# Gate, mixture and attention output kept feature-major in a two-layer trunk on one core

## Chip, core and metric

The kernel runs on one core of one Trainium2 chip. The metric is the device time of one execution in microseconds. Three runs of the kernel before took 431.66, 431.68 and 431.73 us; the median is 431.68 us.

## What is computed

The input is x with 256 tokens of 1024 features, float32. Layer 0 is a causal pooling layer, layer 1 an attention layer with 16 heads of 128 features. Both have a gate. Cut to what matters:

```python
# layer 0: windows 2, 4, 8, 16 over four groups of 512 features
h = rms_norm(x, norm0)
u, z = split(h @ w_in0, 2)                 # 2048 features each
mixed = einsum('bsgc,gcd->bsgd', pooled(u), w_pool0) * pool_scale0
x = x + (mixed * silu(z)) @ w_out0
# layer 1
h = rms_norm(x, norm1)
q, k, v, z = split(h @ w_in1, 4)           # 2048 features each
q, k = rope(rms_norm(q, q_norm1)), rope(rms_norm(k, k_norm1))   # by head
o = softmax(causal(q @ k.T / sqrt(128))) @ v
x = x + (o * silu(z)) @ w_out1
```

All 256 tokens lie in one attention block, so the learned choice of blocks selects nothing further.

## The kernel before

Every large product is made from three products of float32r: high part by high part, high by low, low by high. ScalarE makes the high part of each weight block by a copy (`weight_hi`, L367), VectorE the low part by a subtraction (`weight_lo`, L836). The weights pass through a ring of four slots. A block of 128 x 2048 weights is a granule, and TensorE takes the granules in a fixed order. Granule n = 4g+j belongs to layer 0 (group g of 512 features; j = 0, 1 for u and 2, 3 for z), 16 to 19 to the mixture by w_pool0, 20 to 27 to w_out0, 28+8g+j to layer 1 (pairs of j for q, k, v, z), and 60 to 67 to w_out1. A slot is free for the next high part when TensorE has used it (`w_used`).

`granule` (L599 to L601) is token-major: activations stand still, and 512 weight columns move. `u_granule` (L641 to L644) is feature-major: 128 x 128 weights stand still and 256 tokens move. The results of a group lie in two banks `acc[0]` or two banks `acc[1]`; four further banks `aux` take what is turned (transposed on TensorE, L654), the scores and the attention output.

Layer 0: z is token-major. ScalarE takes tanh with the token's rstd as its scale (L429), VectorE makes the gate from it and the product (L925). GpSimd builds the window sums (L306, L311) from u, VectorE the pooled values (L896) and their low part (L902). The mixture is token-major too; VectorE multiplies it with the gate (L949), and TensorE turns the result (`turn_y0`), since w_out0 needs it feature-major.

Layer 1: ScalarE copies q and k out, squares them by head (L496) and hands the mean (L500) to GpSimd, which makes the norm factors and the rope products (L330 to L348). VectorE adds the rope halves (L1009) and TensorE turns q and k. The attention of group g-1 is spread over the granules of group g (`attend`): scores, maximum on VectorE (`head_max`, L986 to L992), exp on ScalarE (L468, L470), turned probabilities, product with v (L755 to L757), scaling and gate on VectorE (`head_out`), and at the end of the group the turn of y1 (`turn_y1`).

The order of the work is written out by hand on each engine, with semaphores between engines. Every engine takes its list in order, so an instruction that waits holds up all that stands behind it. The queue of the weights issues 66 loads of 1 MB (and the first 2 MB in eight pieces) in this order.

## Time and profile before

| what | value |
|---|---|
| profiled execution, its own time | 431.68 us |
| its span, first to last instruction | 429.9 us |
| TensorE busy | 423.5 us |
| VectorE busy | 281.4 us |
| ScalarE busy | 231.0 us |
| GpSimd busy | 163.1 us |
| mean DMA rate | 175 GB/s |

Times in the profile count from the start of the span. Busy time of TensorE is modelled and overlapping; the start of one matmul to the start of the next is what a matmul costs in the stream. A group of the timeline gives the start, the length from first start to last end and the count. "Idle before" is the time in which the engine stood still just before, with what ended it.

### The profile page before, as it was taken

Reading aid. Unit: us, or ns where it says so; the run is one execution under the profiler, and the core shown is the slowest. Engines: PE = TensorE matmul, PEld = TensorE weight load, DVE = VectorE, ACT = ScalarE, POOL = GpSimd, SP = SyncE. Lnnn points to the kernel's source line nnn. Section 1 sums busy time; section 2 is a strip of 40 time slices with the busy share of each in tenths; the row PEclk is TensorE's granted clock in tenths of the full one; section 3 lists DMA queues with packets and bytes.
Section 4 is the critical chain, followed back from the end, with each engine's and each line's share of the span. In section 5 each row is a group of like instructions: output and inputs, shape, how many; then the busy total and the mean of one; then the engine's idle time right before and its main releaser. Section 6 shows DMA issues by size and latency. Waiting matters only on the chain.

```text
span 429.9 us, 5672 instructions
## 1 busy us (share of the span) xinstructions
PE 423.5 (99%) x2214; PEld 362.7 (84%) x2214; DVE 281.4 (65%) x340; ACT 231.0 (54%) x406; POOL 163.1 (38%) x111
## 2 busy tenths in 40 slices
PE   8999999999999999999999999999999999999997
PEld 8979898988888888888788888888888888888885
DVE  3866898688985544356664798447983579836532
ACT  5745545444554443578447765477654786546310
POOL 0077417267000000089804595055940559300000
PEclk9999999999999999999999999999999999999999
DMA  8987578645455747436833667236672355731002
GB/s 273 386 285 272 195 244 314 214 159 178 167 197 175 217 137 221 123 94 204 295 101 99 186 184 226 91 100 193 196 216 84 99 191 196 246 105 41 2 0 98
DMA packets 38026, 75.25 MB, mean 175 GB/s; under 512 B 1648, under 2 KB 1776, under 8 KB 38000
## 3 DMA queue, kind: packets, MB, share of 16 engines
q1 hardware_dynamic: 37280, 73.83, 52.8%
q10 hardware_dynamic: 720, 1.07, 0.8%
q8 instruction: 17, 0.28, 0.3%
q14 instruction: 9, 0.07, 0.0%
HBM read 73.84 MB, written 1.05 MB: 174 GB/s over the span
## 4 chain that ended last, share of the span: by engine, by line
PE 85%; POOL 7%; DMA 2%; DVE 2%; ACT 1%; SPq 1%; issue 1%; DVEq 0%
PE acc L599 23%; PE acc L601 22%; PE acc L600 22%; PE aux L654 4%; POOL wide L344 3%; PE acc L644 3%; PE acc L643 3%; PE acc L641 3%; DMA raw<-in_w_in_dram 2%; PE aux L738 2%; POOL k_s L337 1%; PE aux L745 1%; SPq L232 1%; PE aux L757 1%; PE aux L756 1%; PE aux L755 1%
## 5 line engine op out<-in xcount | busy, mean ns | idle before, releaser
L836 DVE TENSOR_TENSOR w_lo<-raw,w_hi 128x2048 fp32r<-128x2048 f32 x65 | 165.2, 2548 | 57.6 <-ACT w_hi L367 57.5
L367 ACT ACTIVATE w_hi<-raw 128x2048 fp32r<-128x2048 f32 x64 | 121.9, 1915 | 28.3 <-PE acc L601 21.7
L599 PE MATMUL acc<-w_hi,hT_hi 128*128 128x512 f32 x320 | 127.7, 399 | 1.0 <-DVE w_lo L836 1.0
L601 PE MATMUL acc<-w_hi,hT_lo 128*128 128x512 f32 x320 | 124.9, 390 | 0.0
L600 PE MATMUL acc<-w_lo,hT_hi 128*128 128x512 f32 x320 | 124.6, 389 | 0.0
L601 PEld LDWEIGHTS acc<-w_hi,hT_lo 128*128 128x128 f32 x320 | 60.1, 188 | 13.0
L599 PEld LDWEIGHTS acc<-w_hi,hT_hi 128*128 128x128 f32 x320 | 60.2, 188 | 12.9 <-DVE w_lo L836 1.4
L600 PEld LDWEIGHTS acc<-w_lo,hT_hi 128*128 128x128 f32 x320 | 60.2, 188 | 11.5
L599 PE MATMUL acc<-w_hi,aT_hi 128*128 128x512 f32 x160 | 63.7, 398 | 0.0
L601 PE MATMUL acc<-w_hi,aT_lo 128*128 128x512 f32 x160 | 62.4, 390 | 0.0
L600 PE MATMUL acc<-w_lo,aT_hi 128*128 128x512 f32 x160 | 62.3, 389 | 0.0
L601 PEld LDWEIGHTS acc<-w_hi,aT_lo 128*128 128x128 f32 x160 | 30.0, 188 | 6.4
L600 PEld LDWEIGHTS acc<-w_lo,aT_hi 128*128 128x128 f32 x160 | 30.1, 188 | 5.8
L599 PEld LDWEIGHTS acc<-w_hi,aT_hi 128*128 128x128 f32 x160 | 30.1, 188 | 5.8
L330 POOL TENSOR_TENSOR q_rstd<-qk_mean,minus_half 128x8 f32<-128x8 f32 x4 | 6.6, 1640 | 71.7 <-ACT qk_mean L500 71.7
L986 DVE TENSOR_SCALAR minus_scale<-q_rstd 128x2 f32<-128x2 f32 x16 | 4.3, 266 | 36.6 <-PE aux L738 36.6
L644 PE MATMUL acc<-hT_lo,w_hi 128*128 128x256 f32 x96 | 27.2, 283 | 0.0
L643 PE MATMUL acc<-hT_hi,w_hi 128*128 128x256 f32 x96 | 27.2, 283 | 0.0
L641 PE MATMUL acc<-hT_hi,w_lo 128*128 128x256 f32 x96 | 27.2, 283 | 0.0
L344 POOL TENSOR_TENSOR wide<-k_s,rope_tab 128x256 f32<-128x256 f32 x16 | 25.4, 1616 | 0.3
L318 POOL TENSOR_TENSOR mean<-sumsq 128x2 f32<-128x2 f32 x1 | 0.2, 195 | 65.7 <-ACT ysb L385 65.7
L468 ACT ACTIVATE probs<-aux,exp_bias,q_rstd 128x128 f32<-128x128 f32 x16 | 7.2, 450 | 32.3 <-DVE exp_bias L992 32.3
(125 smaller groups left out, 593.7 us busy)
## 6 DMA issues: line engine op xcount, KB each, us to landing
raw<-in_w_in_dram SPq DMA_DIRECT2D x46, 1024.0 KB, 5.5
raw<-in_w_out_dram SPq DMA_DIRECT2D x16, 1024.0 KB, 5.0
raw<-in_w_pool_dram SPq DMA_DIRECT2D x4, 1024.0 KB, 5.5
raw<-in_w_in_dram SPq DMA_DIRECT2D x8, 256.0 KB, 7.4
wide<-in_xT_dram ACTq DMA_DIRECT2D x4, 256.0 KB, 6.6
xs<-in_x_dram SPq DMA_DIRECT2D x1, 1024.0 KB, 7.7
out_dram<-ysb SPq DMA_DIRECT2D x4, 256.0 KB, 2.0
wide<-in_table_dram SPq DMA_DIRECT2D x1, 256.0 KB, 8.9
```

The source lines that it names most:

```text
L344: ins = pool.tensor_tensor(s4[:, t, :, a:a + half], v4[:, t, :, b:b + half], tab, ALU.mult)
L367: act.activation(w_hi[:, slot, :], raw[:, slot, :], ACT.Copy).then_inc(hi_made, 1)
L468: act.activation(probs[:, 0:P], aux[h % 2][:, 0:P], ACT.Exp, bias=exp_bias[:, h, 0:1], scale=q_rstd[:, g % 2, 0, h:h + 1], accum_out=row_s ...
L599: pe.matmul(a, shi, whi, start=first and k == 0, stop=False)
L600: pe.matmul(a, shi, wlo, start=False, stop=False)
L601: ins = pe.matmul(a, slo, whi, start=False, stop=last and k == GK - 1)
L641: pe.matmul(u_tile(f), wlo, shi, start=j == 0 and k == 0 and f % 2 == 0, stop=False, skip_group_check=True)
L643: pe.matmul(u_tile(f), whi, shi, start=False, stop=False, skip_group_check=True)
L644: ins = pe.matmul(u_tile(f), whi, slo, start=False, stop=end, skip_group_check=True)
L654: ins = pe.transpose(aux[dst_banks[f // 2]][:, c:c + P], src[:, t, f * P:(f + 1) * P], ident[:, :])
L738: pe.matmul(s[:, P:3 * P], qT[:, h, P:SEQ], kT[:, h, :], start=True, stop=True).then_inc(scores_ready, 1)
L836: dve.tensor_tensor(w_lo[:, slot, :], raw[:, slot, :], w_hi[:, slot, :].bitcast(F32), ALU.subtract).then_inc(w_split, 1)
```

## The change

z of layer 0, the mixture, z of layer 1 and the attention output become feature-major. A new helper `tile_of_two` makes a 128-feature tile of them: the low weights meet the high activations (256 columns), and the high weights meet both parts of the activations, which now lie side by side in memory (512 columns). The high parts' product goes into the lower 256 columns of a bank, that with the low activations into the upper 256. The two have to be added afterwards: ScalarE copies the upper part out, VectorE adds it to the lower. A feature-major z has the token's rstd along the columns, so it can't be the scale of an activation any more; VectorE multiplies with a spread copy, `rstd_half_b`, which TensorE spreads once per layer. Tanh comes after it, from SBUF. The scaling by the softmax's sum moves from the attention output to the probabilities before they are turned (`probs_norm`). The turns of y0 and y1 are gone. The z weights of layer 1 are stored in another layout by the host (`w_gate`), in pairs of tiles. The two halves of a bank pair in layer 1 alternate by `side`.

```diff
+        quad = [ctx.enter_context(nc.psum_tensor(f"quad{b}", [P, 4, COLS], F32)) for b in range(2)]
+        acc = [[quad[b][:, t, :] for t in range(TT)] for b in range(2)]
+        aux = [quad[1][:, 2, :], quad[1][:, 3, :], quad[0][:, 2, :], quad[0][:, 3, :]]
...
-                    act.wait_ge(tables_made, 1)
-                for t in range(TT):
-                    product_ready(act, t, 2 * g + 1, 4 * g + 3)
-                    act.activation(wide[:, t, g * COLS:(g + 1) * COLS], acc[1][t][:, :], ACT.Tanh,
-                                   scale=rstd_half[:, t:t + 1]).then_inc(tanh_made, 1)
+                for p in range(2):
+                    product_ready(act, p, 2 * g + 1, 4 * g + 3)
+                    if g > 0:
+                        act.wait_ge(gate_made, 2 * (g - 1) + p + 1)
+                    act.activation(lo_part[p], quad[1][:, 2 * p:2 * p + 2, SEQ:], ACT.Copy).then_inc(lo_copied, 1)
+                for p in range(2):
+                    act.wait_ge(z_made, 2 * g + p + 1)
+                    act.activation(lo_part[p], gateT[:, HPG * g + 2 * p:HPG * g + 2 * p + 2, :],
+                                   ACT.Tanh).then_inc(tanh_made, 1)
...
+            def y0_lo_part(g):
+                for p in range(2):
+                    product_ready(act, p, 8 + g, N_POOL + g)
+                    act.wait_ge(*((y0_summed, 2 * (g - 1) + p + 1) if g else (gate_made, 2 * (GROUPS - 1) + p + 1)))
+                    act.activation(lo_part[p], quad[g % 2][:, 2 * p:2 * p + 2, SEQ:], ACT.Copy).then_inc(lo_copied, 1)
...
+            def z_lo_part(g, p):
+                act.wait_ge(w_used, N_L1 + 8 * g + 6 + p + 1)
+                if g > 0 or p > 0:
+                    act.wait_ge(gate1_made, 2 * g + p)
+                act.activation(z_lo, quad[side(g, 3 + p)][:, 0:2, SEQ:], ACT.Copy).then_inc(z1_lo_copied, 1)
+            def tanh_z(g, p):
+                act.wait_ge(z1_made, 2 * g + p + 1)
+                act.activation(z_lo, gate1T[:, p], ACT.Tanh).then_inc(tanh1_made, 1)
...
+            def tile_of_two(out_, n, c, h, start, stop):
+                pe.matmul(out_[:, 0:SEQ], w_lo[:, n % RING, c:c + P], h[:, 0, :], start=start, stop=False,
+                          skip_group_check=True)
+                return pe.matmul(out_, w_hi[:, n % RING, c:c + P], h.rearrange("p a s -> p (a s)"), start=False,
+                                 stop=stop, skip_group_check=True)
...
+            def mix(g):
+                n = N_POOL + g
+                pe.wait_ge(w_split, n + 1)
+                pe.wait_ge(pooled_split, g + 1)
+                pe.wait_ge(*((u_made, 2 * GROUPS), (z_made, 2 * GROUPS), (y0_summed, 2), (y0_summed, 4))[g])
+                for f in range(HPG):
+                    for k in range(GK):
+                        ins = tile_of_two(quad[g % 2][:, f, :], n, k * COLS + f * P, aT[:, HPG * g + k], k == 0,
+                                          k == GK - 1)
+                    if f == 1:
+                        ins.then_inc(tile0_ready, 1)
+                ins.then_inc(w_used, 1)
...
-                pe.matmul(aux[3][:, 0:P], probsT[:, 0:P], v[0], start=True, stop=True)
-                pe.matmul(aux[3][:, P:2 * P], probsT[:, P:2 * P], v[0], start=True, stop=False)
-                pe.matmul(aux[3][:, P:2 * P], probsT[:, 2 * P:3 * P], v[1], start=False,
-                          stop=True).then_inc(o_ready, 1)
+                o = aux[3][:, 0:SEQ]
+                pe.matmul(o[:, P:SEQ], v[1], probsT[:, SEQ:3 * P], start=True, stop=False, skip_group_check=True)
+                pe.matmul(o, v[0], probsT[:, 0:SEQ], start=False, stop=True, skip_group_check=True).then_inc(o_ready, 1)
...
+            def gate_pair(g, p):
+                n = N_L1 + 8 * g + 6 + p
+                pe.wait_ge(w_split, n + 1)
+                pe.wait_ge(qkv_out[1 + p], TT * (g + 1))
+                for f in range(2):
+                    for k in range(KD):
+                        ins = tile_of_two(acc[side(g, 3 + p)][f], n, k * 2 * P + f * P, hT[:, k], k == 0, k == KD - 1)
+                ins.then_inc(w_used, 1)
...
-                    dve.wait_ge(tanh_made, TT * g + t + 1)
-                    gate = wide[:, t, g * COLS:(g + 1) * COLS]
-                    ins = dve.scalar_tensor_tensor(gate, gate, 1.0, acc[1][t][:, :], ALU.add, ALU.mult)
-                    ins.then_inc(gate_made, 1)
+                if g == 0:
+                    dve.wait_ge(tables_made, 1)
+                for p in range(2):
+                    dve.wait_ge(lo_copied, 2 * g + p + 1)
+                    z = gateT[:, HPG * g + 2 * p:HPG * g + 2 * p + 2, :]
+                    chain.done(dve.tensor_tensor(z, quad[1][:, 2 * p:2 * p + 2, 0:SEQ], lo_part[p], ALU.add))
+                    dve.tensor_tensor(z, z, rstd_half_b[:, :].unsqueeze(1).to_broadcast([P, 2, SEQ]),
+                                      ALU.mult).then_inc(z_made, 1)
+                for p in range(2):
+                    dve.wait_ge(tanh_made, 2 * g + p + 1)
+                    z = gateT[:, HPG * g + 2 * p:HPG * g + 2 * p + 2, :]
+                    dve.scalar_tensor_tensor(z, lo_part[p], 1.0, z, ALU.add, ALU.mult).then_inc(gate_made, 1)
...
+            def y0_out(g):
+                for p in range(2):
+                    dve.wait_ge(lo_copied, 2 * (GROUPS + g) + p + 1)
+                    if g >= 2:
+                        dve.wait_ge(y_split, 2 * (g - 2) + p + 1)
+                    y = y0[g % 2][:, 2 * p:2 * p + 2, :]
+                    dve.tensor_tensor(y, quad[g % 2][:, 2 * p:2 * p + 2, 0:SEQ], lo_part[p],
+                                      ALU.add).then_inc(y0_summed, 1)
+                for p in range(2):
+                    dve.wait_ge(y0_summed, 2 * g + p + 1)
+                    for f in (2 * p, 2 * p + 1):
+                        i = HPG * g + f
+                        ins = dve.scalar_tensor_tensor(y0[g % 2][:, f, :], y0[g % 2][:, f, :],
+                                                       gains[:, 2 * KD + i:2 * KD + i + 1], gateT[:, i, :], ALU.mult,
+                                                       ALU.mult)
+                    ins.then_inc(y0_made, 1)
...
+                y0_out(g)
+                weight_lo(N_POOL + 4 + g, (N_POOL + 4 + g) % RING)
+                y0_lo(g)
...
+            def probs_norm(g, h):
                 dve.wait_ge(exp_made, HPG * g + h + 1)
                 chain.done(dve.reciprocal(row_inv[:, h, :], row_sum[:, h, :]))
-                chain.done(dve.tensor_tensor(o_scale[:, h, :], row_inv[:, h, :], rstd_half[:, :], ALU.mult))
+                dve.tensor_scalar(probs[:, 0:P], probs[:, 0:P], row_inv[:, h, 0:1], 1.0, ALU.mult, ALU.mult)
+                dve.tensor_scalar(probs[:, P:3 * P], probs[:, P:3 * P], row_inv[:, h, 1:2], 1.0, ALU.mult,
+                                  ALU.mult).then_inc(probs_made, 1)
+            def y1_out(g, h):
                 dve.wait_ge(o_ready, HPG * g + h + 1)
-                dve.wait_ge(y_turned, 8 + 2 * g)
-                for t in range(TT):
-                    ins = dve.scalar_tensor_tensor(y1[:, t, h * P:(h + 1) * P], aux[3][:, t * P:(t + 1) * P],
-                                                   o_scale[:, h, t:t + 1], gate1[:, t, h * P:(h + 1) * P],
-                                                   ALU.mult, ALU.mult)
-                ins.then_inc(y1_made, 1)
+                if g > 0:
+                    dve.wait_ge(y_split, 8 + HPG * (g - 1) + h + 1)
+                dve.tensor_tensor(y1T[:, h, :], aux[3][:, 0:SEQ], gate1T[:, h // 2, h % 2, :],
...
+            def z_sum(g, p):
+                dve.wait_ge(z1_lo_copied, 2 * g + p + 1)
+                if g > 0:
+                    dve.wait_ge(y1_made, HPG * (g - 1) + 2 * p + 2)
+                if (g, p) == (0, 0):
+                    dve.wait_ge(rstd_b_made, 2)
+                z = gate1T[:, p]
+                chain.done(dve.tensor_tensor(z, quad[side(g, 3 + p)][:, 0:2, 0:SEQ], z_lo, ALU.add))
+                dve.tensor_tensor(z, z, rstd_half_b[:, :].unsqueeze(1).to_broadcast([P, 2, SEQ]),
+                                  ALU.mult).then_inc(z1_made, 1)
+            def gate_out(g, p):
+                dve.wait_ge(tanh1_made, 2 * g + p + 1)
+                dve.scalar_tensor_tensor(gate1T[:, p], z_lo, 1.0, gate1T[:, p], ALU.add, ALU.mult).then_inc(gate1_made, 1)
...
                 rope_sum(g, 1)
+                z_sum(g, 0)
                 w(7)
-                gate_z(g)
-                if attend:
-                    y1_lo(g - 1)
+                gate_out(g, 0)
```

The change also writes the lists in another order. VectorE in layer 0, between the weights of two groups (`w_lo`), before; L925 makes the gate, L896 and L902 the pooled values, L889 takes u out:

```order
L925 SCALAR_TENSOR_TENSOR wide<-wide,acc 128x512 [waits tanh_made] x2
L836 TENSOR_TENSOR w_lo<-raw,w_hi 128x2048 [waits hi_made] x2
L896 SCALAR_TENSOR_TENSOR k_s<-ysb,uT 128x1024 [waits window_summed]
L889 TENSOR_TENSOR uT<-acc,rstd_b 128x2x256 [waits pooled_made,tile0_ready]
L889 TENSOR_TENSOR uT<-acc,rstd_b 128x2x256 [waits w_used]
L836 TENSOR_TENSOR w_lo<-raw,w_hi 128x2048 [waits hi_made]
L902 TENSOR_TENSOR aT_lo<-k_s,aT_hi 128x1024 [waits pooled_hi]
L836 TENSOR_TENSOR w_lo<-raw,w_hi 128x2048 [waits hi_made]
```

The same place in the changed kernel, where L995 is the addition of the halves, L996 the multiplication and L1001 the gate:

```order
L910 TENSOR_TENSOR w_lo<-raw,w_hi 128x2048 [waits hi_made]
L971 TENSOR_TENSOR aT<-k_s,aT 128x4x256 [waits pooled_hi]
L910 TENSOR_TENSOR w_lo<-raw,w_hi 128x2048 [waits hi_made]
L995 TENSOR_TENSOR wide<-quad,probs_pair 128x512 [waits lo_copied]
L996 TENSOR_TENSOR wide<-wide,rstd_half_b 128x512 [waits dve_chain]
L995 TENSOR_TENSOR wide<-quad,second 128x512 [waits lo_copied]
L996 TENSOR_TENSOR wide<-wide,rstd_half_b 128x512 [waits dve_chain]
L1001 SCALAR_TENSOR_TENSOR wide<-probs_pair,wide 128x512 [waits tanh_made]
L1001 SCALAR_TENSOR_TENSOR wide<-second,wide 128x512 [waits tanh_made]
L910 TENSOR_TENSOR w_lo<-raw,w_hi 128x2048 [waits hi_made] x2
```

Two instructions have become six, at the same place among the weights.

ScalarE in a group of layer 1 with attention, before, from the copy of q to the mean of k. L489 copies a product out, L496 squares, L500 makes the mean, L468 and L470 are exp, L477 copies turned probabilities, L367 is `w_hi`:

```order
L489 ACTIVATE wide<-acc,rstd 128x512 [waits w_used]
L496 ACTIVATE wide,qk_sum<-wide 128x128 [waits q_out]
L496 ACTIVATE wide,qk_sum<-wide 128x128 x7
L500 ACTIVATE qk_mean<-qk_sum 128x8 [waits q_summed]
L367 ACTIVATE w_hi<-raw 128x2048 [waits w_used,raw_landed0]
L468 ACTIVATE probs,row_sum<-aux,exp_bias,q_rstd 128x128 [waits p_turned,bias_made]
L470 ACTIVATE probs,row_sum<-aux,exp_bias,q_rstd 128x256
L477 ACTIVATE probsT<-aux 128x384 [waits p_turned]
L367 ACTIVATE w_hi<-raw 128x2048 [waits w_used,raw_landed1]
```

In the changed kernel (L511 copies out, L518 squares, L523 is the mean, L490 and L492 exp, L499 the probabilities, L383 `w_hi`):

```order
L511 ACTIVATE wide<-quad,rstd 128x512 [waits w_used]
L518 ACTIVATE wide,qk_sum<-wide 128x128 [waits q_out]
L518 ACTIVATE wide,qk_sum<-wide 128x128 x3
L490 ACTIVATE probs_pair,row_sum<-quad,exp_bias,q_rstd 128x128 [waits p_turned,bias_made]
L492 ACTIVATE probs_pair,row_sum<-quad,exp_bias,q_rstd 128x256
L499 ACTIVATE probs_pair<-quad 128x384 [waits p_turned]
L518 ACTIVATE wide,qk_sum<-wide 128x128 [waits q_out]
L518 ACTIVATE wide,qk_sum<-wide 128x128 x3
L523 ACTIVATE qk_mean<-qk_sum 128x8 [waits q_summed]
L383 ACTIVATE w_hi<-raw 128x2048 [waits w_used,raw_landed0]
```

The exp of a head and the copy behind it now stand between the two halves of the squares. The same holds for k, with the exp of head 3.

## Rows read from the trace of the kernel before

**Rows 1.** The page, its first part: busy time of each engine
```profile
PE 423.5 (99%) x2214; PEld 362.7 (84%) x2214; DVE 281.4 (65%) x340; ACT 231.0 (54%) x406; POOL 163.1 (38%) x111
```

**Rows 2.** The cores: span and granted clock
```profile
core 0: 429.9 us, clock 1.000
```

**Rows 3.** Waits of TensorE: total, times, longest us
```profile
PE aux L654 <- DVE k_s L1009: 0.6, 1, 0.6
```

**Rows 4.** Timeline, TensorE: start us, length us, operation, count [idle before]
```profile
31.97 0.28 PE L641 MATMUL acc<-hT_hi,w_lo 128*128 128x256 f32 x1
...
43.49 0.40 PE L599 MATMUL acc<-w_hi,hT_hi 128*128 128x512 f32 x1
...
99.23 0.39 PE L599 MATMUL acc<-w_hi,aT_hi 128*128 128x512 f32 x1
...
110.12 1.04 PE L654 MATMUL aux<-ident,ysb 128*128 128x128 f32 x8
...
116.47 1.03 PE L654 MATMUL aux<-ident,ysb 128*128 128x128 f32 x8
...
267.43 1.04 PE L654 MATMUL aux<-ident,ysb 128*128 128x128 f32 x8
268.31 1.04 PE L654 MATMUL aux<-ident,k_s 128*128 128x128 f32 x8
...
321.35 1.04 PE L654 MATMUL aux<-ident,k_s 128*128 128x128 f32 x8
```

**Rows 5.** Groups of instructions: count, busy us, mean ns, idle before
```profile
L599 PEld LDWEIGHTS acc<-w_hi,hT_hi 128*128 128x128 f32 x320 | 60.2, 188 | 12.9 <-DVE w_lo L836 1.4
...
L864 DVE SCALAR_TENSOR_TENSOR hT_lo<-wide,gains,hT_hi 128x256 fp32r<-128x256 f32 x8 | 3.8, 480 | 0.0
...
L470 ACT ACTIVATE probs<-aux,exp_bias,q_rstd 128x256 f32<-128x256 f32 x16 | 8.9, 554 | 0.0
```

**Rows 6.** Timeline of layer 0: ScalarE, VectorE, GpSimd
```profile
39.64 3.71 ACT L367 ACTIVATE w_hi<-raw 128x2048 fp32r<-128x2048 f32 x2
...
39.21 1.29 DVE L925 SCALAR_TENSOR_TENSOR wide<-wide,acc 128x512 f32<-128x512 f32 x2 [2.90 <-ACT wide L429]
...
55.49 2.41 DVE L836 TENSOR_TENSOR w_lo<-raw,w_hi 128x2048 fp32r<-128x2048 f32 x1
...
64.56 1.22 DVE L896 SCALAR_TENSOR_TENSOR k_s<-qkT,uT 128x1024 f32<-128x1024 f32 x1
...
74.06 3.99 DVE L836 TENSOR_TENSOR w_lo<-raw,w_hi 128x2048 fp32r<-128x2048 f32 x1
...
96.48 3.99 DVE L836 TENSOR_TENSOR w_lo<-raw,w_hi 128x2048 fp32r<-128x2048 f32 x1
...
38.41 1.89 POOL L306 TENSOR_TENSOR ysb<-uT 128x1024 f32<-128x1024 f32 x1
...
98.39 4.33 POOL L306 TENSOR_TENSOR qkT<-ysb 128x1024 f32<-128x1024 f32 x1
```

**Rows 7.** Timeline of layer 1, a group with attention: VectorE, ScalarE
```profile
275.59 0.17 DVE L986 TENSOR_SCALAR minus_scale<-q_rstd 128x2 f32<-128x2 f32 x1 [5.35 <-PE aux L738]
...
281.71 0.17 DVE L986 TENSOR_SCALAR minus_scale<-q_rstd 128x2 f32<-128x2 f32 x1 [2.91 <-PE aux L738]
...
309.69 5.58 DVE L836 TENSOR_TENSOR w_lo<-raw,w_hi 128x2048 fp32r<-128x2048 f32 x2
...
316.47 1.23 DVE L1009 TENSOR_TENSOR k_s<-k_s,wide 128x1024 f32<-128x1024 f32 x1 [1.20 <-POOL k_s L348]
...
276.64 0.46 ACT L468 ACTIVATE probs<-aux,exp_bias,q_rstd 128x128 f32<-128x128 f32 x1 [4.56 <-DVE exp_bias L992]
...
281.71 0.31 ACT L496 ACTIVATE wide<-wide 128x128 f32<-128x128 f32 x1
...
284.19 0.21 ACT L500 ACTIVATE qk_mean<-qk_sum 128x8 f32<-128x8 f32 x1
...
297.78 0.21 ACT L500 ACTIVATE qk_mean<-qk_sum 128x8 f32<-128x8 f32 x1
```

More of the change, by code:

```diff
@@ L108, in bass_hybrid_trunk @@
         rstd_b = sb("rstd_b", [P, SEQ])
+        rstd_half_b = sb("rstd_half_b", [P, SEQ])
+        second = sb("second", [P, 2 * SEQ])
         diag = sb("diag", [P, TT, P])
@@ L249, in _ @@
             for g in range(GROUPS):
-                for j in range(8):
+                for j in range(6):
                     src = w_in1_v[:, (j % 2) * GK:(j % 2 + 1) * GK, bass.ds((j // 2) * D_INNER + g * COLS, COLS)]
                     load(j % RING, src, N_L1 + 8 * g + j)
+                for p in range(2):
+                    load((6 + p) % RING, w_gate[2 * g + p].rearrange("p (k n) -> p k n", k=GK), N_L1 + 8 * g + 6 + p)
             for i, (h, q) in enumerate(OUT1_ORDER):
@@ L689, in layer0 @@
                     u_granule(g, 1)
[L690 to L693 removed]
+                z_granule(g, 0)
+                z_granule(g, 1)
             for g in range(GROUPS):
                 layer0(g)
[L699 to L703 removed]
             pe.wait_ge(ident_made, 1)
             for g in range(GROUPS):
[L707 to L711 removed]
+                mix(g)
             def turn_x1(half):
                 pe.wait_ge(x1_made, TT * (half + 1))
+                pe.wait_ge(y0_summed, 2 * GROUPS)
                 turn((2 * half, 2 * half + 1), xs[:, :, half * COLS:(half + 1) * COLS], h_turned)
@@ L796, in layer1 @@
                         attend(g - 1, j)
-                    if j == 6:
-                        turn_qk(g, 0, first)
-                    if j == 7:
-                        if not first:
-                            turn_y1(g - 1, g)
-                        turn_qk(g, 1, first)
+                    if first and j == 3:
+                        spread_rstd(1)
+                gate_pair(g, 0)
+                turn_qk(g, 0, first)
+                gate_pair(g, 1)
+                turn_qk(g, 1, first)
             layer1(0, first=True)
@@ new lines, in layer1 @@
+                w(1)
+                if g == 0:
+                    dve.wait_ge(rstd_made, 2)
+                    for t in range(TT):
+                        ins = dve.tensor_scalar(diag[:, t, :], ident[:, :], rstd[:, t:t + 1], 1.0, ALU.mult, ALU.mult)
+                    ins.then_inc(diag_made, 1)
+                if g > 0:
+                    head_max(b, 2)
+                    y1_out(b, 0)
+                    probs_norm(b, 2)
+                w(2)
+                if g > 0:
+                    y1_rest(b, 0)
+                    head_max(b, 3)
+                    y1_out(b, 1)
+                    probs_norm(b, 3)
@@ L1075, in _ @@
-            y1_lo_bank(last, 1)
+            z_sum(last, 1)
+            weight_lo(N_OUT1 + 3, 3)
+            gate_out(last, 1)
+            head_max(last, 0)
+            probs_norm(last, 0)
+            weight_lo(N_OUT1 + 4, 0)
+            head_max(last, 1)
+            probs_norm(last, 1)
+            weight_lo(N_OUT1 + 5, 1)
+            head_max(last, 2)
+            y1_out(last, 0)
+            probs_norm(last, 2)
+            weight_lo(N_OUT1 + 6, 2)
+            y1_rest(last, 0)
+            head_max(last, 3)
@@ L1076, in _ @@
+            y1_out(last, 1)
+            probs_norm(last, 3)
+            weight_lo(N_OUT1 + 7, 3)
+            y1_rest(last, 1)
+            y1_out(last, 2)
+            y1_rest(last, 2)
+            y1_out(last, 3)
+            y1_rest(last, 3)
             for half in range(2):
                 for t in range(TT):
-                    product_ready(dve, t, 30 + half, N_OUT1 + 6 + half)
-                    dve.wait_ge(y_turned, 16)
+                    product_ready(dve, t, 26 + half, N_OUT1 + 6 + half)
```

366 lines of the change are left out of this document (173 added, 193 removed).

## The prediction

> **What bounds the kernel now.** I read the page's first part before all else: TensorE is busy for 423.5 of 429.9 us, the others far less [rows 1]. Its granted clock is 1.000 over the whole span [rows 2]. The waits of TensorE come next: they can't sum to more than the missing 6.4 us, and the only one late in the program is 0.6 us, at a turn of k [rows 3]. So a change pays by what it takes out of TensorE's own stream, as long as nothing else becomes late. The price in that stream is the distance between starts in the timeline, not the busy time of a matmul (which overlaps the next). 96 matmuls of 256 columns start between 31.97 and 43.49: 0.120 us each. 48 of 512 columns start between 99.23 and 110.12: 0.2269 us each [rows 4]. The two give 0.4176 ns a column, which is 2.4 GHz, and 0.0132 us a matmul on top. Last I read what VectorE, ScalarE and GpSimd do in a group of each layer [rows 6, 7], because the change lengthens their chains.
>
> **TensorE's stream.** A granule before is 24 matmuls of 512 columns (12,288 columns). Where the change has a pair (256 columns by the low weights, 512 by the high ones) a granule is 16 pairs: again 12,288 columns, but 32 matmuls. It costs 8 x 0.0132 = 0.107 us more, and there are 8 gate granules of layer 0, 4 mixture granules and 8 gate granules of layer 1: +2.1 us. The second spreading of rstd adds 4 matmuls of 128 columns, half of what 8 transposes take: +0.45. Gone are the turns. A mixture granule with a turn takes 116.47 - 110.12 = 6.35 us against 10.89 / 2 = 5.445 without: 0.905 for each of four, -3.6. Three turns of y1 beside that of k cost 268.31 - 267.43 = 0.88 each, -2.6, and the two halves of one at the end about 0.5 each with the switch, -1.0 [rows 4]. The attention output has 2 products for 3 over the same columns, two passes less a head: 16 x 2 x 0.0132 = -0.4. Sum -5.0 us, if TensorE waits no more than before. What isn't shown before is a 256-column matmul behind one of 512: its weights take 0.188 us to load [rows 5], hidden now at distances of 0.120. The bounds are 0.120 and 0.188, at most 320 x 0.068 = 21.8 us; I take 0.120, the nearer row, since behind 512 columns there is more time to hide a load.
>
> **Layer 0, the gate's new chain.** Before, a gate product costs VectorE one pass per half, 1.29 us for both, after a tanh straight from PSUM. Now ScalarE copies the low part, VectorE adds and multiplies for each half, ScalarE takes tanh, VectorE makes the gate, and only then ScalarE goes on with the weights of granule 4g+7. A pass over 512 columns starts 0.60 us after the one before, 0.70 after one whose result it needs (from the 1.29 for two): four are 2.7 us [rows 6]. Call T(g) the time at which the second half of z is scaled, which frees the gate's banks.
> First group: VectorE must wait for GpSimd's tables (until its next operation starts, 38.41), as they share the area. The multiplication has both operands in SBUF, and GpSimd's 1.89 us operation runs until 40.30. So from 40.30: 0.60 + 0.70 + 0.70, T(0) = 42.3 [rows 6].
> From the start of the w_hi copy at 39.64 to the end of w_lo at 57.90 the old chain runs 18.3 us, with ScalarE, VectorE and GpSimd handing on to each other. It now starts one tanh after T(0), at 42.95; the end is 61.3, T(1) = 64.0.
> After T(1): tanh 0.65, w_hi 1.9, two w_lo 4.45, so the w_lo of granule 12 ends at 71.0. From there (64.56 before) to the end of the w_lo of granule 14 (78.05) is 13.5 us, of which GpSimd's window sums block a good part. Hence T(2) = 71.0 + 13.5 + 2.9 = 87.4. The same again ends at 107.9; an add, then GpSimd's last sum, which ends 2.25 us after that point (102.72 against 100.47), holds the multiplication to 110.2, and T(3) = 112.2 [rows 6].
> TensorE reaches the second mixture granule at 99.23 + 0.8 + 5.55 = 105.6. It writes the banks that T(3) frees: a wait of 6.6 us. Groups 1 and 2 are just in time (TensorE wants T(1) at 66.2 and T(2) at 88.8).
> That an add (one operand in PSUM) isn't held is shown by the row at 39.21: two such passes take 1.29 us under GpSimd's operation. w_lo, with two SBUF operands, stretches from 2.25 to 3.3 when GpSimd runs: 5.58 for two [rows 7]. The Trainium skill (SBUF — State Buffer, Who interferes with whom) says that a VectorE instruction with two SBUF inputs and a GpSimd one that reads SBUF block each other whole, while one SBUF input doesn't contend; the trace agrees, and by it the change adds just the kind of pass that is exposed.
>
> **The mixture.** After T(3): tanh 0.65, w_hi 1.9, w_lo 2.25, pooled 1.2, ScalarE's copy 1.1, its rest 1.2, two adds 1.3: the first mixture is read out at 121.8, for which the third mixture granule waits (TensorE is free at 117.8). From then on VectorE sets the pace: two adds 1.25, four scalings of 256 columns 1.6 (0.48 long, 0.39 apart [rows 5]), a w_lo 2.2, two rests 1.2, together 6.25 us a group against 5.55 of TensorE. So mixture granule 3 starts at 128.1, the first output granule at 134.4, the second at 139.9. Before, that one starts at about 130.1. Layer 0 costs +9.8 us instead of the -2.3 of TensorE's stream.
>
> **Layer 1.** The group without attention: GpSimd's chain of q and k is untouched, k is ready at the same point, then the bank of the first gate half must be scaled (1.4 us) before the next group begins, of which a turn of 0.9 covers most. +0.4.
> A group with attention, counted from its first granule (269.2 before; period 321.35 - 268.31 = 53.04 [rows 4]). VectorE sees the scores of head 1 at 12.5 in both. Before, ScalarE squares q at once (2.4 us for eight), q's mean is made at 15.0 and k's at 28.6. Now between the halves of q's squares stand the exp of head 1 (1.0) and a copy (0.4): the mean comes 1.5 later. The next w_hi and w_lo slide with it, so head 2's exp ends at 24.2. Then a copy 0.4, w_hi 1.9, the first y1 copy 0.35, k's two copies 1.2 and four squares 1.2: 29.2. Head 3's exp has its bias at 30.1 (a w_lo from 26.5, y1's rest 0.35 and a maximum of 1.05 are ahead of it); exp 1.0, copy 0.35, four squares and the mean 1.5: k's mean is made at 33.0, 4.4 us later than before. From k's mean to the end of rope's sum was 317.7 - 297.8 = 19.9 us, in which VectorE and GpSimd alternate all the way [rows 7]. It stays four w_lo, one rope sum and GpSimd's nine operations, plus three rests of y1 (0.4 each, and some waiting): 21.5. So k is roped at 54.5, while TensorE wants to turn it at 51.6 (and not before 52.5, as the last values product waits about 0.9 for the read-out of head 2, which stands behind a w_lo). Then VectorE scales the gate half, 1.5, beside the turn, and the next group starts at 56.0: +3.0 us for each of three, +9.0. The score of head 1 at 12.5 meets ScalarE and VectorE in step again, so the lag doesn't grow.
> The end: the turns save 1.0, the first turn of probabilities waits 0.5 for the new normalisation: -0.5.
>
> **Sum.** +9.8 + 0.4 + 9.0 - 0.5 = +18.7 us. The profiled execution took 431.68 us, 1.78 outside its span of 429.9, and is the median run itself: 431.7 + 18.7 = 450.4 us.
>
> **Rivals.**
> TensorE alone decides (faster): the chains keep up, and -5.0 gives 426.7. For it speak VectorE's 65% and ScalarE's 54% [rows 1]; against it, that TensorE waits for a given bank and not for an average. It decides where the two chains together bring less than 5 us of waits: T(3) by 105.6 and k's mean by about 30.
> Only layer 0's chain binds: 450.4 - 9.0 - 1.0 = 440.4, if ScalarE's new order delays k by less than the 3 us of slack that there was.
> Only layer 1's binds: 431.7 - 2.3 + 0.4 + 9.0 - 0.5 = 438.3, if VectorE regains the lag of the first group.
> The pair of widths costs its upper bound: TensorE's stream is then 17 us longer than now, much of it beneath the waits; 450 to 460.
> The clock falls in the wait of 6.6 us, and the next granules run at 1.2 GHz: a granule of pairs takes 5.1 us more by the price of a column. The first one mostly fits into the 4 us that TensorE would wait anyway (+1), a second costs 5: 452 to 457. No wait of the trace is long enough to support or exclude it. The Trainium skill (TensorE: Matmul & The Clock Gate, What's actually happening) says that the clock stands at half after idleness and that activity releases it; by that rule this rival should happen.
>
> **Chances.** Forecast 0.54, layer 0 alone 0.14, layer 1 alone 0.06, TensorE alone 0.12, the clock 0.10, the widths 0.04. About 0.2% (0.9 us) is what a measurement tells from no change. Faster 0.12 (TensorE alone), same 0.03 (a part of the cases with one chain, half as strong), slower 0.85. The range goes from 438, layer 1 alone, to 457, the clock's end.
>
> **What would show it.** TensorE waits some 7 us before the second mixture granule, released by VectorE's multiplication with rstd_half_b, and 0.7 to 4 us before the next three; in each of the three attention groups it waits 2 us at the turn of k, released by VectorE's rope sum, and 0.5 after it. Pairs start 0.347 us apart. VectorE's busy time rises by some 20 us. The forecast falls if T(3) comes before 106, if k's mean comes less than 2 us later than now, or if a pair takes more than 0.36 us.

## The result and the profile after

The changed kernel takes 444.52 us (median of 4 runs, 444.42 to 444.86) against 431.71 of the kernel before (4 runs): a ratio of 1.0297, with a 95% interval from 1.028 to 1.0315. It is slower, by 12.8 us. 450.4 was forecast, with a range from 438 to 457.

The profiled execution took 444.42 us over a span of 442.3. The page of the kernel after, first the busy shares, then TensorE's and VectorE's slices and the granted clock:

```profile
PE 425.1 (96%) x2282; PEld 365.3 (83%) x2282; DVE 317.1 (72%) x390; ACT 240.6 (54%) x432; POOL 156.8 (35%) x111
...
PE   9999999996799999999999999999999999999997
...
DVE  3867888979799755436774869838698387986632
...
PEclk9999999999799999999999999999999999999999
```

TensorE is busy for 1.6 us more than before [rows 1], a slow stretch included, so most of the 12.4 us by which the span grew are waits of TensorE. One dip stands in its slices 10 and 11 (from 99 to 122 us), and in the second of them the granted clock falls: 0.50 from 109.3 to 116.1, 1.00 before and behind. All waits of TensorE (kernel after; us in total, times, longest):

```profile
PE quad L704 <- DVE wide L996: 5.0, 1, 5.0
PE quad L836 <- DVE ysb L1087: 2.0, 3, 0.8
PE quad L704 <- DVE ysb L1016: 1.9, 2, 1.5
PE quad L749 <- DVE k_s L1097: 1.8, 3, 0.6
PE quad L758 <- DVE k_s L905: 1.0, 1, 1.0
PE quad L704 <- DVE w_lo L910: 1.0, 1, 1.0
PE quad L651 <- DVE wide L1107: 0.9, 4, 0.2
PE quad L651 <- issue: 0.3, 1, 0.3
```

Where [rows 3] had one late wait, there are fourteen. L996 is the multiplication of z, L1016 the add that reads out a mixture, L1087 the read-out of an attention head, L1097 the rope sum, L1107 the multiplication of z in layer 1. The two waits of 1.0 are at the start and in both kernels.

The places in time, which answer to [rows 4] (start us, length us, count, [idle before]). L749 turns x1 and k; a line of L651 behind a turn of k opens the next group of layer 1, the last one the output granules. TensorE after:

```profile
111.44 0.55 PE L704 MATMUL quad<-aT,w_lo 128*128 128x256 f32 x1 [4.98 <-DVE wide L996]
...
112.21 0.41 PE L704 MATMUL quad<-aT,w_lo 128*128 128x256 f32 x1
...
116.05 0.34 PE L704 MATMUL quad<-aT,w_lo 128*128 128x256 f32 x1
...
116.47 0.28 PE L704 MATMUL quad<-aT,w_lo 128*128 128x256 f32 x1
...
116.81 0.28 PE L704 MATMUL quad<-aT,w_lo 128*128 128x256 f32 x1
...
160.55 1.03 PE L749 MATMUL quad<-ident,xs 128*128 128x128 f32 x8
...
225.13 0.50 PE L651 MATMUL quad<-w_hi,hT 128*128 128x512 f32 x1 [0.23 <-DVE wide L1107]
...
278.42 1.09 PE L749 MATMUL quad<-ident,k_s 128*128 128x128 f32 x8 [0.64 <-DVE k_s L1097]
...
279.74 0.50 PE L651 MATMUL quad<-w_hi,hT 128*128 128x512 f32 x1 [0.23 <-DVE wide L1107]
...
388.47 0.50 PE L651 MATMUL quad<-w_hi,aT 128*128 128x512 f32 x1 [0.23 <-DVE wide L1107]
```

The same places before:

```profile
151.82 1.04 PE L654 MATMUL aux<-ident,xs 128*128 128x128 f32 x8
...
216.06 0.47 PE L599 MATMUL acc<-w_hi,hT_hi 128*128 128x512 f32 x1
...
269.10 0.47 PE L599 MATMUL acc<-w_hi,hT_hi 128*128 128x512 f32 x1
...
375.18 0.47 PE L599 MATMUL acc<-w_hi,aT_hi 128*128 128x512 f32 x1
```

These give the ledger, in us:

| stretch, up to | before | after | longer by |
|---|---|---|---|
| first turn of x1, which closes layer 0 | 151.82 | 160.55 | 8.7 |
| end of the group without attention | 216.06 | 225.13 | 0.3 |
| end of the first group with attention | 269.10 | 279.74 | 1.6 |
| end of the two others | 375.18 | 388.47 | 2.6 (1.3 each) |
| end of the span | 429.9 | 442.3 | -0.9 |

Before rounding they sum to 12.4, and 0.3 more lies outside the span.

The pairs of the second mixture granule start 0.64 us apart from 111.8 to 116.1 and 0.35 after. The 768 columns of a pair take 0.64 us at 1.2 GHz and 0.32 at 2.4, so these are the two levels of the clock. The granule takes 8.0 us instead of 5.65, but the next one has to wait for VectorE (L1016) anyway, and still waits 1.5.

### The profile page after: what moved, and what is told of

It reads as the page before. It is cut to its first block, busy times and chain, and to the rows that moved or that the text cites. A ratio compares the mean times of both kernels' runs of the same rounds, so it can differ in the third digit from the quotient of the medians.

```text
span 442.3 us, 5897 instructions
## 1 busy us (share of the span) xinstructions
PE 425.1 (96%) x2282; PEld 365.3 (83%) x2282; DVE 317.1 (72%) x390; ACT 240.6 (54%) x432; POOL 156.8 (35%) x111
## 4 chain that ended last, share of the span: by engine, by line
PE 49%; DVE 20%; ACT 11%; issue 9%; POOL 7%; DMA 2%; SPq 1%; ACTq 0%; DVEq 0%
PE quad L651 10%; PE quad L653 10%; PE quad L652 10%; DVE w_lo L910 7%; PE quad L706 6%; ACT w_hi L383 5%; PE quad L704 3%; POOL wide L360 3%; DVE aT L1092 3%; PE quad L693 3%; PE quad L696 3%; ACT wide L518 3%; PE quad L695 3%; DMA raw<-in_w_in_dram 2%; POOL k_s L353 1%
## 5 line engine op out<-in xcount | busy, mean ns | idle before, releaser
L383 ACT ACTIVATE w_hi<-raw 128x2048 fp32r<-128x2048 f32 x64 | 121.4, 1910 | 14.2 <-PE quad L653 14.2
L706 PE MATMUL quad<-hT,w_hi 128*128 128x512 f32 x256 | 90.5, 396 | 0.0
L651 PE MATMUL quad<-w_hi,hT 128*128 128x512 f32 x192 | 76.9, 400 | 0.7 <-DVE wide L1107 0.7
L653 PE MATMUL quad<-w_hi,hT 128*128 128x512 f32 x192 | 74.9, 390 | 0.0
L652 PE MATMUL quad<-w_lo,hT 128*128 128x512 f32 x192 | 74.8, 390 | 0.0
L704 PE MATMUL quad<-hT,w_lo 128*128 128x256 f32 x256 | 73.0, 285 | 1.0 <-DVE w_lo L910 1.0
L706 PEld LDWEIGHTS quad<-hT,w_hi 128*128 128x128 f32 x256 | 48.1, 188 | 10.9
L651 PE MATMUL quad<-w_hi,aT 128*128 128x512 f32 x128 | 50.8, 397 | 0.6 <-issue 0.3
L653 PE MATMUL quad<-w_hi,aT 128*128 128x512 f32 x128 | 49.9, 390 | 0.0
L652 PE MATMUL quad<-w_lo,aT 128*128 128x512 f32 x128 | 49.8, 389 | 0.0
L704 PEld LDWEIGHTS quad<-hT,w_lo 128*128 128x128 f32 x256 | 48.4, 189 | 1.4 <-DVE w_lo L910 1.3
L651 PEld LDWEIGHTS quad<-w_hi,hT 128*128 128x128 f32 x192 | 36.1, 188 | 8.4 <-DVE wide L1107 1.4
L653 PEld LDWEIGHTS quad<-w_hi,hT 128*128 128x128 f32 x192 | 36.0, 188 | 7.6
L490 ACT ACTIVATE probs_pair<-quad,exp_bias,q_rstd 128x128 f32<-128x128 f32 x16 | 7.3, 458 | 40.8 <-DVE exp_bias L1073 40.8
L651 PEld LDWEIGHTS quad<-w_hi,aT 128*128 128x128 f32 x128 | 24.0, 188 | 5.9 <-issue 0.6
L653 PEld LDWEIGHTS quad<-w_hi,aT 128*128 128x128 f32 x128 | 24.0, 188 | 5.1
L693 PE MATMUL quad<-hT,w_lo 128*128 128x256 f32 x96 | 27.2, 283 | 0.0
```

Of the source, the lines that this page charges most:

```text
L383: act.activation(w_hi[:, slot, :], raw[:, slot, :], ACT.Copy).then_inc(hi_made, 1)
L651: pe.matmul(a, shi, whi, start=first and k == 0, stop=False)
L652: pe.matmul(a, shi, wlo, start=False, stop=False)
L653: ins = pe.matmul(a, slo, whi, start=False, stop=last and k == GK - 1)
L693: pe.matmul(u_tile(f), wlo, shi, start=j == 0 and k == 0 and f % 2 == 0, stop=False, skip_group_check=True)
L704: pe.matmul(out_[:, 0:SEQ], w_lo[:, n % RING, c:c + P], h[:, 0, :], start=start, stop=False, skip_group_check=True)
```

## The experiments

**One layer alone.** The changed kernel with layer 1 and the end of the kernel before:

```diff
-                for j in range(6):
+                for j in range(8):
                     src = w_in1_v[:, (j % 2) * GK:(j % 2 + 1) * GK, bass.ds((j // 2) * D_INNER + g * COLS, COLS)]
                     load(j % RING, src, N_L1 + 8 * g + j)
-                for p in range(2):
-                    load((6 + p) % RING, w_gate[2 * g + p].rearrange("p (k n) -> p k n", k=GK), N_L1 + 8 * g + 6 + p)
```

and on ScalarE, TensorE and VectorE all from the first attention helper on is the code before, with y1 and the gate token-major and y1's turns.

> Layer 0 of the changed kernel, layer 1 and its end as in the kernel before (w_in1 loaded as before too). Theory: the two layers' prices are independent. The traces give layer 0 as the difference of the first turn of x1, 160.55 - 151.82 = +8.7 us, so 431.7 + 8.7 = 440.4, and the wait of 5.0 before the second mixture granule is there unchanged. Rival: part of layer 0's lag is taken up by slack in the old layer 1, or it leaves something late there (weights, banks): then the time is off 440.4 by more than 1 us, towards 438 or 442.

Measured: 440.56 us (440.44 to 440.84), ratio 1.0198 [1.0177, 1.0219]. That was the expectation (440.4). The wait of 5.0 is there, the turn of x1 is at 160.62. Layer 0 costs 8.8 us by itself and layer 1 the other 4.0; no slack of the old layer 1 takes any of it up.

**z first (VectorE, layer 0).**

```diff
-                weight_lo(4 * g + 6, 2)
                 for p in range(2):
                     dve.wait_ge(lo_copied, 2 * g + p + 1)
...
+                weight_lo(4 * g + 6, 2)
```

> The changed kernel with one reorder on VectorE in each group of layer 0: the add and the multiplication of z stand ahead of the w_lo of granule 4g+6, not behind it. Theory 'order' (the wait before the second mixture granule is there because z queues behind a w_lo of 3.99 us): ScalarE's copies end at 101.4, VectorE is free at 103.2, z is scaled by about 107.5, the wait falls from 5.0 to about 1.5, and the time by 3.5 us to 441.0. Rival 'GpSimd' (the multiplication has both operands in SBUF, and GpSimd's window sums run without a break from 102.3 to 110.2): z is scaled no sooner than about 110, the time falls by 1 us at most. Rival 'mixture pace' (VectorE's 6.18 us a group sets the first output granule wherever the wait is): the wait goes down, the later waits of the mixture grow by as much, and the time stays within 0.5.

Measured: 438.16 us (438.09 to 438.31), 6.4 less. VectorE of the changed kernel, and then of this one:

```profile
100.39 2.91 DVE L971 TENSOR_TENSOR aT<-k_s,aT 128x1024 fp32r<-128x1024 f32 x1
103.22 3.99 DVE L910 TENSOR_TENSOR w_lo<-raw,w_hi 128x2048 fp32r<-128x2048 f32 x1
...
107.85 2.11 DVE L996 TENSOR_TENSOR wide<-wide,rstd_half_b 128x512 f32<-128x512 f32 x1
...
110.60 0.69 DVE L996 TENSOR_TENSOR wide<-wide,rstd_half_b 128x512 f32<-128x512 f32 x1
...
119.49 0.68 DVE L1016 TENSOR_TENSOR ysb<-quad,probs_pair 128x512 f32<-128x512 f32 x1
```

```profile
95.68 2.91 DVE L971 TENSOR_TENSOR aT<-k_s,aT 128x1024 fp32r<-128x1024 f32 x1
...
102.42 1.29 DVE L995 TENSOR_TENSOR wide<-wide,rstd_half_b 128x512 f32<-128x512 f32 x1
103.64 2.41 DVE L910 TENSOR_TENSOR w_lo<-raw,w_hi 128x2048 fp32r<-128x2048 f32 x1
...
112.86 0.68 DVE L1016 TENSOR_TENSOR ysb<-quad,probs_pair 128x512 f32<-128x512 f32 x1
```

z of the fourth group is scaled at 103.7, not 111.3. The rest of the third pooled product (L971), which nobody moved, is 4.7 us earlier too: the chain of the first groups had carried its lag along. The order theory holds, but the gain is nearly double the 3.5 that was expected, and its rivals (1 us at most, or none) fall. The wait of 5.0 is gone, and one of 1.9 stands before the third mixture granule. The first read of a mixture (L1016) moves by 6.6 and the time by 6.4: that row, not the wait of 5.0, is what sets the end of layer 0.

**z in PSUM.**

```diff
-                    chain.done(dve.tensor_tensor(z, quad[1][:, 2 * p:2 * p + 2, 0:SEQ], lo_part[p], ALU.add))
-                    dve.tensor_tensor(z, z, rstd_half_b[:, :].unsqueeze(1).to_broadcast([P, 2, SEQ]),
+                    zq = quad[1][:, 2 * p:2 * p + 2, 0:SEQ]
+                    chain.done(dve.tensor_tensor(zq, zq, lo_part[p], ALU.add))
+                    dve.tensor_tensor(z, zq, rstd_half_b[:, :].unsqueeze(1).to_broadcast([P, 2, SEQ]),
```

> The changed kernel with the add of z written back into PSUM, in place, and the multiplication read from there, so that it has only one operand in SBUF. Order of instructions unchanged. Theory 'GpSimd blocks the multiplication': the pass at 107.85 falls from 2.11 to 0.69, as do that at 39.32 (1.64) in the first group; z of the fourth group is scaled 1.4 us sooner, the wait is 3.6 in place of 5.0, the time 443.1. Rival 'order' only: the block was a chance overlap, or the write into PSUM costs as much (TensorE works on other banks): within 0.4 of 444.5.

Measured: 442.61 us median, 442.34 to 443.76 (1.9 less, where 1.4 was expected). VectorE, then TensorE of this run:

```profile
106.95 0.69 DVE L997 TENSOR_TENSOR wide<-quad,rstd_half_b 128x512 f32<-128x512 f32 x1
```

```profile
109.12 0.36 PE L704 MATMUL quad<-aT,w_lo 128*128 128x256 f32 x1 [2.59 <-DVE wide L997]
...
118.59 0.55 PE L704 MATMUL quad<-aT,w_lo 128*128 128x256 f32 x1 [3.59 <-DVE ysb L1017]
119.37 0.41 PE L704 MATMUL quad<-aT,w_lo 128*128 128x256 f32 x1
...
123.85 0.41 PE L704 MATMUL quad<-aT,w_lo 128*128 128x256 f32 x1
124.44 0.28 PE L704 MATMUL quad<-aT,w_lo 128*128 128x256 f32 x1
```

The pass falls from 2.11 to 0.69 with an operand in PSUM, beside the same sums of GpSimd: the blocking is a matter of two SBUF operands, as the Trainium skill has it (SBUF — State Buffer, Who interferes with whom). In the changed kernel the blocked pass ended at 109.96, some 0.5 us after GpSimd's sum (109.42). The same pass of the first group falls from 1.64 to 0.69 too, so the chain is 0.9 earlier from there on and the wait before the second granule is 2.6, not the 3.6 that was expected. In this profile the clock doesn't fall at that wait but in the next one, of 3.6, and there it isn't covered: the granule at 118.59 runs at 1.2 GHz until 124.4, and none waits behind it. That execution is the 443.76; the three others of the same kernel are 442.34 to 442.72, with clocks of 0.992 to 0.995. Where it fell in those isn't seen. The likely reading, not shown, is that the slow clock costs 1.2 us where no wait follows, and little where one does.

**k's squares together (ScalarE, layer 1).**

```diff
                 square_heads(g, 1, 0)
+                square_heads(g, 1, 1)
                 if g > 0:
                     exp_scores(b, 3)
                     probs_out(b, 2)
-                square_heads(g, 1, 1)
```

> The changed kernel with one reorder on ScalarE in each group of layer 1: k's eight squares stand together, ahead of head 3's exp and the copy of head 2's probabilities, not four on either side. Theory (k's mean comes late because of that order, and all of VectorE's and GpSimd's tail moves with it): the mean 2.2 us earlier, the waits at the three turns of k (0.64, 0.64, 0.52) and the three of 0.23 before the next group go: -2.5 us, 442.0. Rival 'tail': VectorE's own passes (rests of y1 and w_lo beside GpSimd) set the end of the rope sum, the mean matters less than 1 us, and the time falls by less than 0.8. Rival 'exchange': head 3's exp, 1.2 us later, makes its turn of probabilities late: a new wait of about 1 us a group, and the time stays.

Measured: 438.04 us (437.84 to 438.17), 6.5 less where 2.5 was expected. k's mean, from the start of its group, stands at 32.7 in the changed kernel and at 30.3 here; first ScalarE and VectorE of the changed kernel, then of this one, and its TensorE:

```profile
312.43 0.21 ACT L523 ACTIVATE qk_mean<-qk_sum 128x8 f32<-128x8 f32 x1
...
318.73 0.41 DVE L1087 TENSOR_TENSOR ysb<-quad,wide 128x256 f32<-128x256 f32 x1
...
331.52 1.21 DVE L1097 TENSOR_TENSOR k_s<-k_s,wide 128x1024 f32<-128x1024 f32 x1
```

```profile
308.11 0.21 ACT L523 ACTIVATE qk_mean<-qk_sum 128x8 f32<-128x8 f32 x1
...
315.19 0.41 DVE L1087 TENSOR_TENSOR ysb<-quad,wide 128x256 f32<-128x256 f32 x1
...
327.45 1.21 DVE L1097 TENSOR_TENSOR k_s<-k_s,wide 128x1024 f32<-128x1024 f32 x1
...
276.83 1.04 PE L749 MATMUL quad<-ident,k_s 128*128 128x128 f32 x8
...
329.29 1.03 PE L749 MATMUL quad<-ident,k_s 128*128 128x128 f32 x8
```

The turns of k wait no more, and are 52.46 and 52.18 apart (54.37 and 54.36 in the changed kernel). Two things had been left out of the expectation. The w_hi and w_lo behind the squares come earlier too, and with them the read-out of head 2 (L1087), so those waits (2.0) vanish as well. And a wait costs more than its row says: idle time counts from the modelled end of the matmul before, 0.39 after its start, while the next could start 0.23 after it. So each wait at a turn of k or at the product of an attention head costs 0.16 more; at the start of the next group, behind a turn, it is up to 0.24. By the distances of starts in the two kernels the nine waits cost 6.0 of the 6.5, where their rows list 1.8 + 2.0 + 0.7 = 4.5. The last 0.5 isn't accounted for. Neither rival happened: the mean counts for more than 1 us, and no new wait came at the turned probabilities.

**Both reorders.** The two diffs above in one kernel.

> The changed kernel with both reorders: z ahead of the w_lo on VectorE in layer 0, k's squares together on ScalarE in layer 1. Alone they measured -6.4 and -6.5 us. Theory: the two places are independent, 444.5 - 6.4 - 6.5 = 431.6, as much as the kernel before (431.75), and all the waits left are 1.9 in the mixture and some 2 at the start. Rival: the gains overlap (the lag that layer 0 hands to layer 1 is part of what the second reorder took out): 433 to 435.

Measured: 431.66 us (12 runs), ratio 0.9994 [0.998, 1.0007]: no different from the kernel before. The two places are independent (431.6 by the sum), so these two orders account for the whole 12.8 us. A wait of 2.0 is left before the third mixture granule. The mean clock is 1.0 in three of the twelve runs (431.21 to 431.31 us) and 0.995 or 0.996 in the nine others (median 431.73, one of them 431.32): some 0.4 us. The profiled execution is one of the three, with the wait of 2.0 and a clock of 1.00 all through it.

**The first mixture read out first.** On VectorE (y0_sums are y0_out's adds, y0_scale its scalings; ScalarE's copy of the low part moves likewise), with both reorders and once alone:

```diff
-            pooled_out(GROUPS - 1)
-            pooled_rest(GROUPS - 1)
...
-                y0_out(g)
+                if g == 0:
+                    dve.wait_ge(window_summed, GROUPS)
+                y0_sums(g)
+                if g == 0:
+                    pooled_out(GROUPS - 1)
+                y0_scale(g)
+                if g == 0:
+                    pooled_rest(GROUPS - 1)
```

> As the run with both reorders, and the first mixture is read out (ScalarE's copy, VectorE's two adds) ahead of the last pooled product's mean, copy and rest. Theory (the wait of 1.9 before the third mixture granule stands there because its bank's read-out queues behind the pooled chain, from 109.4 to 112.9): the adds end at about 110 in place of 114, that wait goes, no other comes, and the time is 1.9 to 2.3 us below the run with both, 429.5; that is below the kernel before. Rival 'mixture pace' (VectorE's 6.2 us a group against TensorE's 5.65 sets the first output granules): the wait moves to the fourth mixture granule (pooled rest) or to the first output granules, and less than 0.8 us is gained.

> The changed kernel with only the first mixture's read-out moved ahead of the last pooled product. Theory (the wait of 5.0 before the second mixture granule is z's alone; the read-out of the first mixture decides the third and so the end of layer 0): the wait of 5.0 stays, that of 1.5 goes, 0.4 too; the second granule runs in part at 1.2 GHz as before, now with less slack under it. The time falls by 1.0 to 1.9 us to 443. Rival 'clock' (the 2.4 us that the slow granule costs were hidden in those waits and now show): the time stays within 0.5 of 444.5.

With both reorders: 430.06 us (12 runs), ratio 0.996 [0.9947, 0.9973], 1.6 less than without, where 1.9 to 2.3 was expected. Alone on the changed kernel: 443.6 (443.4 to 443.74), 0.9 less, just under the 1.0 to 1.9 of the theory and more than the clock's rival allowed; the wait of 5.0 stays (4.9), and one of 1.9 stands before the fourth granule. The adds of the first mixture start at 109.25 in place of 112.8, but a wait of 1.65 is left, one granule on (waits of TensorE, with both reorders):

```profile
PE quad L704 <- DVE ysb L1014: 1.7, 1, 1.7
```

It is the read-out of the second mixture, at 118.01 behind a w_lo and two rests. The theory was half right: the wait before the third granule went, but one nearly as long came before the fourth, handed to the next in the queue.

**Every mixture read out first.** The copy and the adds of mixture g+1 also go ahead of the w_hi and w_lo of output granule g:

```diff
-                y0_sums(g)
-                if g == 0:
+                    y0_sums(0)
                     pooled_out(GROUPS - 1)
...
                 if g == 0:
                     pooled_rest(GROUPS - 1)
+                if g < GROUPS - 1:
+                    y0_sums(g + 1)
                 weight_lo(N_POOL + 4 + g, (N_POOL + 4 + g) % RING)
                 y0_lo(g)
```

> As the run with both reorders and the first mixture read out early, and each later mixture's copy and adds also stand ahead of the w_hi and w_lo of the output weights. Theory (the 1.65 left before the fourth mixture granule is the read-out of the second mixture queued behind a w_lo of 2.29 and two rests): that wait and the 0.35 before the first output granule go, nothing takes their place, since VectorE's surplus over TensorE then only delays what is wanted later: 430.06 - 2.0 = 428.1. Rival 'pace' (VectorE needs 6.2 us a group where TensorE needs 5.65, so work must be late somewhere): the wait comes back before the third or fourth output granule, and less than 0.8 us is gained.

Measured: 427.52 us (6 runs, five of them 427.37 to 427.65 and one 431.43), ratio 0.9902 [0.9865, 0.9939]: 1% below the kernel before, and 2.5 less than with only the first mixture read out early. All of TensorE's waits in this kernel:

```profile
PE quad L760 <- DVE k_s L907: 1.0, 1, 1.0
PE quad L706 <- DVE w_lo L912: 1.0, 1, 1.0
PE quad L653 <- DVE wide L1117: 0.2, 1, 0.2
```

The rival 'pace' falls: VectorE's 6.2 us a group in the mixture, against 5.65 of TensorE, holds nobody up if it does first what is wanted first.

**One w_lo earlier at the start.** VectorE makes the w_lo of the fourth granule before it waits for the sums of squares, not after:

```diff
+            weight_lo(3, 3)
             dve.wait_ge(sumT_made, 1)
...
                 if g == 0:
-                    weight_lo(3, 3)
```

> As the run before it, and the w_lo of the fourth granule stands ahead of VectorE's wait for the sums of squares (it idles 2.3 us there). The wait of 0.95 at 26.0, which the kernel before has too (0.96), goes: 1.0 us less, 427.1. Rival: the norm's chain (diag, rstd_b) is next and TensorE waits as long for it a granule later: no change.

Measured: 426.47 us (6 runs, 426.32 to 427.84), ratio 0.9864 [0.9839, 0.9889], the fastest. The second wait of 1.0 is gone from the list. This one isn't owed to the change: the kernel before has the same wait, and would probably gain as much; that wasn't run.

**Layer 0 repaired, layer 1 as before.** Layer 0 is that of the kernel with every mixture read out first, layer 1 and the end are those of the kernel before.

> Layer 0 of the changed kernel with its two reorders (z first, mixture's read-out first), layer 1 and end as in the kernel before. Theory: with the waits gone, layer 0 is worth what it takes out of TensorE's stream, -3.6 for the turns and +1.3 for 12 granules of pairs: 431.75 - 2.3 = 429.4. Rival: layer 0's feature-major form gains nothing even so, as what is left (waits, the longer chain at the first group) eats it: 431 to 432, and all of the repaired kernel's gain is layer 1's.

Measured: 430.5 us (10 runs), ratio 0.9954 [0.9934, 0.9974]: layer 0 gains 1.4, between the theory (2.3) and its rival (0.8 at most). Of TensorE's waits in layer 0 only those at the start, which the kernel before has too, are left. What is missing fits the distance of pairs (TensorE with every mixture read out first, layer 0; then layer 1 with attention):

```profile
43.70 0.28 PE L706 MATMUL quad<-hT,w_lo 128*128 128x256 f32 x1
...
49.01 0.28 PE L706 MATMUL quad<-hT,w_lo 128*128 128x256 f32 x1
...
254.87 0.28 PE L706 MATMUL quad<-hT,w_lo 128*128 128x256 f32 x1
...
259.73 0.28 PE L706 MATMUL quad<-hT,w_lo 128*128 128x256 f32 x1
```

15 distances in 5.31 us are 0.354, 14 in 4.86 are 0.347. The forecast took 0.347 for all. 12 granules x 16 x 0.006 = 1.2 us, about what is missing: the turn of x1 is 1.2 earlier than before (150.62), not 2.3.

## Why the prediction was right, and where it was off

The side, the places and the releasers were right: the chains of VectorE and ScalarE, not TensorE's stream, decide. The terms:

- Layer 0, +9.8 forecast, +8.7 measured. T(g) was forecast as 42.3, 64.0, 87.4, 112.2 and came as 42.3, 63.8, 86.8, 111.3; the wait of 6.6 was 5.0, the first output granule 134.4 was 133.2. VectorE's pace in the mixture, 6.25 forecast, is 6.18. The path was right as well: the prediction put the end of layer 0 behind the first mixture's read-out (121.8 forecast, 120.8 measured) and the pace from there on, not behind the wait of 6.6. What it left out is that the length of this queue is a matter of order alone: read out first, the same passes at the same pace hold nobody up.
- The first group of layer 1, +0.4 forecast, +0.3 measured.
- A group with attention, +3.0 forecast; +1.6 for the first and +1.3 for each of the two others measured, 4.2 in place of 9.0. This is the term that was mis-sized, and most of the 5.9 us between forecast and result. k's mean was forecast at 33.0 and came at 32.7 (second of the three groups). But "three rests of y1 (0.4 each, and some waiting): 21.5" came as 20.3 (312.43 to 332.73, against 19.9 before [rows 7]). The three rests take 1.26, 0.95 and 1.52 there and still add only 0.4. VectorE and GpSimd alternate, and a pass more on one of them probably fits mostly beside the other; no run isolates that. The closing part, 1.5, was 1.3.
- The waits there were named rightly; the one at the turn of k, where the lag of k shows, was 0.5 to 0.6 and not 2. The others were near: read-out of head 2 0.6 to 0.8 (0.9 forecast), next group 0.2 (0.5 forecast).
- The end, -0.5 forecast, -0.9 measured.
- VectorE's busy time rose by 36 us, not 20, with 50 passes more (390 for 340 [rows 1]). That it has 28% of its time left says nothing: the place of the passes counts.
- "TensorE alone decides", 426.7: not in this order of work, but it is about what the change is worth. With three pieces of order mended the kernel takes 427.5. The 0.8 that is missing is the distance of pairs in layer 0 (1.2), less a wait of 0.6 at a turn of k that became one of 0.2.
- The clock did fall, and the rival that gave 452 to 457 was wrong on the price. The slow stretch ended inside the second mixture granule, which became 2.35 us longer and not 5.1, and no other granule was slow. The next one had to wait for VectorE anyway. By the Trainium skill (TensorE: Matmul & The Clock Gate, What's actually happening) idleness brings the half clock; the runs agree only in part. The clock fell in the wait of 5.0 (all four executions of the changed kernel have a mean of 0.992) and right behind the wait of 1.9 with z first (0.50 from 115.1 to 118.4, four executions at 0.995 or 0.996). It stayed at 1.00 through the wait of 2.6 with z in PSUM and through the 2.0 of the profiled execution with both reorders. It costs what isn't covered.

What stays open is why pairs are 0.353 apart on average in some places and 0.347 in others, while triples of 512 columns are 0.680 apart everywhere. It isn't the place in the program. The fourth mixture granule runs at 0.347 in the changed kernel and at 0.353 with z in PSUM or with every mixture read out first. In the mixture of every kernel here, at the full clock, the distance changes only where the stream was interrupted by a wait: with k's squares together it is 0.353 in the first granule, 0.347 behind the wait of 4.9, 0.353 behind that of 1.3 and 0.347 behind that of 0.3.

## What to carry to other kernels

When a change moves work from the bound engine to another, ask for each new pass what stands ahead of it in that engine's queue and who is waiting. Here the change cost 12.8 us, because in layer 0 passes that TensorE waited for stood behind weight splitting that nobody needed yet, and in layer 1 k's squares stood behind an exp and a copy. With the same passes in another order it gained 4.3. Put read-outs that free a bank ahead of work for later granules, and keep the operations that feed the slowest chain (k's mean) together. A wait's row understates its cost by the overlap of the matmul before it (0.16 us or more here), and removing a wait moves it to the next in the queue until that one is put first too.

## What the runs showed of the hardware

- A VectorE pass with both operands in SBUF took 1.3 to 2.1 us beside GpSimd's sums and 0.69 with one of them in PSUM, at the same place.
- The granted clock fell to 0.5 in or right behind waits of TensorE of 1.9, 3.6 and 5.0 us, and stayed at 1.00 through profiled waits of 2.0 and 2.6. In the changed kernel its cost doesn't show; with both reorders it was some 0.4 us, and with z in PSUM probably 1.2.
- A pair of 256 and 512 columns starts 0.347 or 0.353 us after the one before, so loading weights (0.188 us) for a 256-column matmul behind one of 512 is nearly or wholly hidden. Which of the two it is changed in the mixture only at a wait.
